# One step of a two-layer hybrid decoder on one core: boundary order, the last chunk's samples, states in the index keys' place, 25 projection blocks

## The reference, cut to what matters

```python
for l in range(DEPTH):
    mod = (silu_c @ p['w_ada'][l] + p['b_ada'][l]).reshape(B, N_MOD, D)
    hh = modulate(rmsnorm(x, g_pre[l, 0]), m[0], m[1])
    x = x + 0.5 * m[2] * rmsnorm(swiglu(hh, ...), g_post[l, 0])
    ...                      # mixer of the layer, then a second SwiGLU
```

```python
    inner = jnp.einsum('bhij,bjhv->bihv', att, vb)
    cross = jnp.einsum('bihd,bhdv->bihv', qb, s) * q_dec[None, :, :, None]
    s = s * c_dec[None, :, None, None] + jnp.einsum('bjhd,bjhv->bhdv', kb * k_dec[None, :, :, None], vb)
```

## Time and profile before

| what | value |
|---|---|
| median of 3 runs (lowest, highest) | 1372.47 us (1371.24, 1377.88) |
| the profiled execution's own time | 1372.95 us |
| its span (first to last instruction) | 1371.3 us |
| busy PE, DVE, ACT, POOL | 1333.3, 787.0, 623.6, 110.8 us |
| granted TensorE clock, mean | 0.998 of full |
| DMA | 260.00 MB, mean 190 GB/s |

### The profile page before, as it was taken

The page is one execution under the profiler, slowest core; times in us unless marked ns, Lnnn a source line. Parts: engine busy times, 40 slices in busy tenths (PEclk is TensorE's granted clock), DMA queues, the critical chain, the costliest instruction groups (busy, mean ns, idle before and its releaser), DMA issues.

```text
span 1371.3 us, 24418 instructions
## 1 busy us (share of the span) xinstructions
PE 1333.3 (97%) x9776; PEld 1254.5 (91%) x9776; DVE 787.0 (57%) x1432; ACT 623.6 (45%) x1068; POOL 110.8 (8%) x199
## 2 busy tenths in 40 slices
PE   6999999999999999999999999999998999999998
PEld 4899999989976789999999899999987989999997
DVE  5444444576787885445455644445576895444443
ACT  5433333463533555344344534334467665333332
POOL 0100000032011111000000200000020110000000
PEclk9999999999999999999999999999999999999999
DMA  9865646456359756554544546444564843444342
GB/s 361 300 213 188 214 159 241 154 172 225 123 201 349 279 196 224 183 186 142 200 149 158 209 146 227 154 167 158 168 221 141 293 154 123 153 150 147 127 146 83
DMA packets 79459, 260.00 MB, mean 190 GB/s; under 512 B 10626, under 2 KB 20930, under 8 KB 78210
## 3 DMA queue, kind: packets, MB, share of 16 engines
q1 hardware_dynamic: 62882, 199.50, 43.3%
q0 software_dynamic: 16480, 59.15, 11.8%
HBM read 254.39 MB, written 4.23 MB: 189 GB/s over the span
## 4 chain that ended last, share of the span: by engine, by line
PE 87%; DVE 5%; DMA 4%; ACT 2%; issue 1%; SPq 1%; POOL 0%; DVEq 0%; ACTq 0%
PE ps L1701 27%; PE ps L1702 26%; PE ps L1703 26%; PE ps L1769 2%; DMA lent_lo<-in_ada 2%; DMA front<-in_front 1%; DVE w_lo L2274 1%; DVE f L2359 1%; DVE f L2342 1%; DMA w_raw<-in_pj 1%; ACT w_hi L2052 1%; DVE x L2346 0%; DMA st_in<-in_state_ret 0%; DVE f L2364 0%; PE ps L1318 0%
## 5 line engine op out<-in xcount | busy, mean ns | idle before, releaser
L1701 PE MATMUL ps<-xn_hi,w_hi 128*128 128x320 f32 x1808 | 569.3, 315 | 11.7 <-DVE xn_lo L2354 7.5
L1703 PE MATMUL ps<-xn_hi,w_lo 128*128 128x320 f32 x1808 | 559.4, 309 | 0.0
L1702 PE MATMUL ps<-xn_lo,w_hi 128*128 128x320 f32 x1808 | 559.2, 309 | 0.0
L2274 DVE TENSOR_TENSOR w_lo<-w_raw,w_hi 128x1024 fp32r<-128x1024 f32 (+1 forms) x357 | 383.1, 1110 | 121.4 <-ACT w_hi L2052 120.9
L2052 ACT ACTIVATE w_hi<-w_raw 128x1024 fp32r<-128x1024 f32 x362 | 331.5, 961 | 81.7 <-PE ps L1703 74.3
L1701 PEld LDWEIGHTS ps<-xn_hi,w_hi 128*128 128x128 f32 x1808 | 340.0, 188 | 28.0 <-DVE xn_lo L2354 10.9
L1702 PEld LDWEIGHTS ps<-xn_lo,w_hi 128*128 128x128 f32 x1808 | 340.3, 188 | 0.9
L1703 PEld LDWEIGHTS ps<-xn_hi,w_lo 128*128 128x128 f32 x1808 | 340.0, 188 | 0.0
L1701 PE MATMUL ps<-mid_hi,w_hi 128*128 128x320 f32 x704 | 217.9, 310 | 0.3 <-DVE w_lo L2274 0.3
L1702 PE MATMUL ps<-mid_lo,w_hi 128*128 128x320 f32 x704 | 217.2, 308 | 0.0
L1703 PE MATMUL ps<-mid_hi,w_lo 128*128 128x320 f32 x704 | 217.2, 308 | 0.0
(11 more groups left out here) (321 smaller groups left out, 1045.1 us busy)
## 6 DMA issues: line engine op xcount, KB each, us to landing
w_raw<-in_gu SPq DMA_DIRECT2D x176, 512.0 KB, 4.7
a_raw<-in_ada POOLq DMA_DIRECT2D x76, 512.0 KB, 7.3
w_raw<-in_down SPq DMA_DIRECT2D x64, 512.0 KB, 3.6
w_raw<-in_pj SPq DMA_DIRECT2D x58, 512.0 KB, 5.0
w_raw<-in_down SPq DMA_DIRECT2D x64, 192.0 KB, 3.6
ex_xn<-in_ada POOLq DMA_DIRECT2D x16, 512.0 KB, 5.8
w_raw<-in_ada SPq DMA_DIRECT2D x16, 512.0 KB, 5.9
front<-in_front SPq DMA_DIRECT2D x5, 1024.0 KB, 12.4
```

What stands on the lines that cost most here:

```text
L1701: pe.matmul(out, hi, xhi, start=start, stop=False)
L1702: pe.matmul(out, hi, xlo, start=False, stop=False)
L1703: return pe.matmul(out, w_lo[s][:, w_at:w_at + P], xhi, start=False, stop=stop)
L2274: dve.tensor_tensor(w_lo[s][:, cols], w_raw[:, s, cols], w_hi[s][:, cols].bitcast(F32), ALU.subtract).then_inc(w_split, 1)
```

## The change

It has these parts. (1) Boundaries: `two_tiles` takes a written order (`FIRST_TILES`): after chunks 0 and 1 of tile 0 come chunks 0 and 1 of the first block of tile 1, then chunk 2 of tile 0 and the second block of tile 1; from chunk 4 on the order is the old one. (2) The last chunk's samples go from POOL to DVE: the scale stands before `low(6)`, the shift behind it. (3) even_in has 25 blocks: wi shares block 7 with ki (ACT writes three pieces out of it), rv of head 0 is block 9, the last tile is a half (and 8 columns, which the copy takes along). (4) The states of heads 0, 1 and 3 land where the index keys lay (`cached[:, :, 0, :]`), those of heads 0 and 1 from the fifth `ix_done` on, that of head 2 in `st_in`; SP's wait for `st_landed` goes. (5) `cross`: q times old state is made with 32 columns of q as weights and the state as the moving side, eight products into PSUM rows of 32, copied by ACT (`xs`), then two products with a selection matrix (`sel_x`, a new constant). (6) DVE's rounds for the samples: 1 at b = 22, then 4, 3, 1 in heads 0, 1, 2; at b = 24 the prompt's rounds and mask stand before the weight split. PE's `logits(0)` stands before the wait for all blocks. (7) odd_in: ACT loads the sigmoid's table ahead, and its `gates` stand before the weight splits. (8) gate0's first pieces stand at tile 2, not 3. (9) `out_projection`: ACT's wait for the gate factors stands behind the first weight split. (10) `stat_last`: the token sums stand before the products with x.

```diff
-EVEN_BLOCKS = 26
+EVEN_BLOCKS, EVEN_SLOTS = 25, 26
+HALF_TILE = 1024 + 8
+def even_slot(b):
+    if b == 9:
+        return B_RV
+    return b if b < B_RV else b + 1
-ADA_PLAN += [("gate0", c, 4) for c in (3, 7, 11, 15, 19)] + [("down0", 1, 4)]
+ADA_PLAN += [("gate0", c, 4) for c in (2, 7, 11, 15, 19)] + [("down0", 1, 4)]
+BOTH = (0, 1)
+FIRST_TILES = [(0, 0, BOTH), (0, 1, BOTH), (1, 0, (0,)), (1, 1, (0,)), (0, 2, BOTH), (1, 0, (1,)), (0, 3, BOTH),
+               (1, 1, (1,)), (0, 4, BOTH), (1, 2, BOTH), (0, 5, BOTH), (1, 3, BOTH), (0, 6, BOTH), (1, 4, BOTH),
+               (0, 7, BOTH), (1, 5, BOTH), (1, 6, BOTH), (1, 7, BOTH)]
-            for k in range(2, KC):
+            for k in range(2, KC - 1):
                 samples(gp, stage, k)
+        def state_of(h):
+            past = cached[:, :, 0, P * (h % 2):P * (h % 2 + 1)]
+            return st_in[:, :, :] if h == 2 else past
...
+            gp.wait_ge(ix_done, 5)
+            load_state(0)
+            load_state(1)
             gp.wait_ge(p_evac, PB + EVEN_BLOCKS)
             gp.wait_ge(rope_done, CR + 16)
+            gp.dma_start(t["k_o"], proj[:, B_K, :]).then_inc(kvo_stored, 16)
...
             for h in range(RH):
+                if h < RH - 2:
+                    gp.wait_ge(st_ready, h + 1)
+                    gp.wait_ge(o_done, h + 1)
+                    load_state(h + 2)
+                store_states(gp, h)
...
                 turn(2 * h)
+                pe.wait_ge(qd_ready, h + 2)
+                pe.wait_ge(st_landed[h % 2], 16 * (h // 2 + 1))
+                for b in range(NB):
+                    a, rows = b // 4, slice(32 * (b % 4), 32 * (b % 4 + 1))
+                    last = pe.matmul(ps[rows, a, 0:P], qz[:, NT * b:NT * b + 32], state_of(h)[:, b, :], start=True,
+                                     stop=True)
+                last.then_inc(xs_done, 1)
...
                 pe.wait_ge(vm_ready, h + 1)
+                pe.wait_ge(xs_ready, h + 1)
...
-                pe.wait_ge(st_landed, 16 * (h + 1))
-                for b in range(NB):
-                    pe.matmul(ps[:, 3, PTOK:TOK], st_in[:, b, :], qz[:, STOK * b:STOK * (b + 1)],
-                              start=(b == 0), stop=False)
+                for a in range(2):
+                    pe.matmul(ps[:, 3, PTOK:TOK], xs[:, a, :], sel_x[:, a, :], start=(a == 0), stop=False)
...
-            pe.wait_ge(p_evac, PB + EVEN_BLOCKS)
             pe.wait_ge(rope_done, CR + 16)
             logits(0)
+            pe.wait_ge(p_evac, PB + EVEN_BLOCKS)
...
+                    if b + h == B_KI:
+                        for to in (0, HD):
+                            act.activation(proj[to:to + HD, B_KI, :], ps[0:HD, 2 * j + h, 0:TOK], ACT.Copy)
+                        act.activation(proj[0:32, B_WI, :], ps[HD:HD + 32, 2 * j + h, 0:TOK], ACT.Copy).then_inc(p_evac, 1)
+                        continue
...
                 turned(2 * h)
+                act.wait_ge(xs_done, h + 1)
+                act.activation(xs[:, :, :], ps[:, 0:2, 0:P], ACT.Copy).then_inc(xs_ready, 1)
                 exponents(2 * h + 1)
...
+                if b == 24:
+                    top(scores[1], 2)
+                    mask(scores[1], bias_p[:, 1, :])
                 if b != 8:
                     n = base + b // 2 + (2 if b < 8 else 1)
-                    split_w(n, n % 2)
+                    split_w(n, n % 2, HALF_TILE if n == base + EVEN_IN_TILES - 1 else 2048)
...
-            dve.memset(qz[:, :], 0.0).then_inc(qd_ready, 1)
+            dve.memset(qz[:, STOK:STOK + 32], 0.0).then_inc(qd_ready, 1)
...
-                if h < 2:
-                    top(score_s[:, :], score_rounds // 3)
-                elif h == 2:
+                if h < RH - 1:
+                    top(score_s[:, :], late_rounds[h])
+                if h == RH - 2:
                     mask(score_s[:, :], bias_s[:, :])
...
             ada_copy(14)
+            act.activation(warm[:, :], eps[:, :], ACT.Sigmoid)
...
             evacuate_x(4)
+            gates(0)
             split_half(4, 0)
-            gates(0)
             evacuate_x(5)
             split_half(4, 1)
             gates(1)
+            gates(2)
             evacuate_x(6)
             split_half(5, 0)
-            gates(2)
             gates(3)
...
                             sp_.wait_ge(w_used, CR + W_BASE["even_out"])
-                            sp_.wait_ge(st_landed, 16)
...
             def stat_last(stage):
-                pe.wait_ge(x_ready, 8 * 5)
-                pe.wait_ge(row_ready, A_UNITS)
-                for k, bank in PE_ADDS.items():
-                    pe.matmul(ps[:, bank, 0:TOK], ident[:, :], x[:, k, :], start=True, stop=False)
                 pe.wait_ge(y_evac, CR + 8 * SUB[stage] + 7)
                 token_sums(B_YSUM, 0, sqacc[:, :], True, False)
                 pe.wait_ge(sq_ready, 8 * (SUB[stage] + 1))
                 token_sums(B_YSUM, 0, sq2[:, 1, :], False, True).then_inc(stat_done, 1)
+                pe.wait_ge(x_ready, 8 * 5)
+                pe.wait_ge(row_ready, A_UNITS)
+                old(0)
                 spread(y_stat(stage), ry3, B_RY)
+                old(1)
+                grown(0)
...
             def out_projection(stage, done):
-                act.wait_ge(coef_ready, 2 * SUB[stage] + 2)
...
+                    if i == 0:
+                        act.wait_ge(coef_ready, 2 * SUB[stage] + 2)
                     act.wait_ge(half_used, done + i + 1)
...
                         scaled(k)
+                        if k == KC - 1:
+                            sample_scale(k)
                         low(k - 1)
+                    dve.wait_ge(xmod_ready, 8 * sub + KC - 1)
+                    sample_shift(KC - 1)
                     low(KC - 1)
```

More of the change, by code:

```diff
@@ L315, in build @@
         sel_s = pb("sel_s", [P, 2, STOK])
+        sel_x = pb("sel_x", [P, 2, STOK])
         hmask = pb("hmask", [P, NIH])
@@ L365, in build @@
         w_used = sem("w_used")
-        fr_landed = [sem(f"fr_landed{c}") for c in range(KC)]
         fr_row, fr_sel, fr_mod = sem("fr_row"), sem("fr_sel"), sem("fr_mod")
@@ L898, in evacuate @@
                 if t_:
-                    split_w(base + t_ + 1, (base + j + 1) % 2)
-                for h in range(2):
-                    if h == 0:
+                    split_w(base + t_ + 1, (base + j + 1) % 2, HALF_TILE if t_ + 2 == EVEN_IN_TILES else 2048)
+                for h in range(len(kinds)):
+                    if h == 0 and len(kinds) == 2:
                         act.wait_ge(half_used, t_ + 1)
@@ L917, in act_even @@
             for b in range(0, EVEN_BLOCKS, 2):
-                kinds = ((plain, key) if B_RQK <= b < B_RQK + 8 else
-                         ((ACT.Silu, 1.0),) * 2 if b >= B_RG else (plain, plain))
+                kinds = tuple(key if B_RQK <= q < B_RQK + 8 and q % 2 else
+                              (ACT.Silu, 1.0) if even_slot(q) >= B_RG else plain
+                              for q in range(b, min(b + 2, EVEN_BLOCKS)))
                 evacuate(b // 2, b // 2 % 2, b, kinds)
@@ L1645, in proj_loads @@
                 for i in tiles:
-                    load_w(t["pj"], first_tile + i, W_BASE[stage] + i)
+                    half = stage == "even_in" and i == EVEN_IN_TILES - 1
+                    load_w(t["pj"], first_tile + i, W_BASE[stage] + i, HALF_TILE if half else 2048)
             def lent_loads():
@@ L1736, in two_tiles @@
                         pe.wait_ge(xn_ready, 8 * PREP[stage] + k + 1)
-                    for b in range(2):
+                    for b in blocks:
                         if k == 0:
@@ L1891, in stat_last @@
                 token_sums(B_YSUM, 0, sq2[:, 1, :], False, True).then_inc(stat_done, 1)
+                pe.wait_ge(x_ready, 8 * 5)
+                pe.wait_ge(row_ready, A_UNITS)
+                old(0)
                 spread(y_stat(stage), ry3, B_RY)
-                for k, bank in PE_ADDS.items():
-                    pe.wait_ge(y_grown, k + 1 + k % 2)
-                    pe.matmul(ps[:, bank, 0:TOK], ident[:, :], f[:, k, :], start=False, stop=True).then_inc(y_sum, 1)
+                old(1)
+                grown(0)
+                old(3)
+                grown(1)
+                grown(3)
             def ff_sums(stage):
@@ L2761, in tables @@
     out["sel_s"], out["rep_s"] = sel, sel.transpose(2, 1, 0)
+    out["sel_x"] = sel * (xx == 0)[:, None, None]
     head = 2 * (xx % 2) + xx // 2
```

99 lines of the change are left out of this document (50 added, 49 removed).

## The result

The changed kernel takes 1360.03 us (median of 4 runs, 1357.74 to 1360.75), the kernel before on the same chip 1372.95 (4 runs, 1371.24 to 1377.88). The ratio is 0.990, 95% interval 0.987 to 0.9925.

What follows compares the result with a forecast made beforehand. PE, busy 97% of the span, bounds the kernel. Terms -1.2 - 3.5 - 0.75 - 4.2 - 0.4 - 5.3 - 1.6 + 1.25 = -15.7 us on 1372.95 give 1357.25, forecast as 1356.8 for the median; range 1352 to 1361.5.

Steps and rivals of the forecast that it cites:

- Boundaries: At five boundaries: the written order removes no wait, and chunk 7's scale delays low(6); +0.25 us each, +1.25 in all.
- gate0: Before gate0's tile 2: 16 moved products fill PE's idle 1.12 us and its short stall; -1.2 us.
- even_in and the entry: even_in: one block less, -3.5 us; entry to the heads: fewer DVE rounds and less memset before logits(0), -0.75 us.
- The heads: Attention heads: cheaper cross -3.6, no waits for w_ada pieces -1.2, DVE's later rounds and states +0.6; -4.2 us.
- rival (a): Attention stage: the DMA queue binds, PE keeps a 0.6 us wait in two heads; +1.3, 1358.1 us; chance 0.14.
- even_out: Before even_out's second tile: PE's 1.27 us wait for a bank shrinks as ACT and DVE split sooner; -0.4 us.
- odd_in: odd_in: gate waits go, -3.6 us, and the time lost to a lowered clock behind them, -1.7; -5.3 us.
- The table load: odd_in: ACT's 1.28 us sigmoid table load fits in 1.35 us of idle time, delaying the next high part 0.2 at most.
- The end: Kernel end: 1.61 us of products no longer stand before the token sums; -1.6 us.
- (b): Boundaries: each gains 0.44 us from the written order instead of losing 0.25; 1353.3 us; chance 0.13.
- (c): odd_in: DVE's 31 us run starts when it did and holds back the 5.3 us gain; 1362.1 us; chance 0.10.
- (d): Attention stage: TensorE's clock falls, making the kernel slower than before, 1417 us if throughout; chance 0.03.

Runs made afterwards that it cites:

- experiments 9 and 10: The kernel before with only chunk 7's samples moved to DVE, and the kernel before with only part 7: ratios to before 1.0005 and 0.9975.
- experiments 1 and 2: Changed kernel with chunk 7's samples back on POOL, median 1357.39 us; changed kernel with low(6) ahead of sample_scale(7), median 1357.94 us.
- experiment 3: Changed kernel with two_tiles in the old order at the boundaries, chunk 7's samples still on DVE: median 1359.73 us, ratio to before 0.990.
- experiment 8: Changed kernel with the old products of q with the old state and the wide qz memset: median 1362.40 us, ratio to before 0.993.
- Part 7 alone: The kernel before with only part 7 (sigmoid table loaded ahead, gates ahead of weight halves): median 1368.50 us, ratio to before 0.9975.
- odd_undone: Changed kernel with part 7 undone (no early sigmoid table load, gates behind the weight halves): median 1362.65 us, odd stretch 113.14 us.
- odd_no_order: Changed kernel with the early sigmoid table load kept but the gates behind the weight halves again: median 1361.48 us, odd stretch 112.22 us.
- before_part2: The kernel before with only chunk 7's samples moved to DVE at all five boundaries: median 1372.14 us, ratio to before 1.0005.
- experiments 5 to 7: Changed kernel with part 7 undone, without its early table load, and without its new gate order: medians 1362.65, 1361.62 and 1361.48 us.
- odd_no_table: Changed kernel without the early load of the sigmoid's table, gates in their new order: median 1361.62 us, odd stretch 110.50 us.
- best2: best1 with added products on PE at the start to warm it: median 1361.12 us.
- best1: Changed kernel with low(6) ahead of sample_scale(7) and head 2's state loaded early into the relu buffer: median 1358.92 us, ratio to before 0.992.

## Why the prediction came out right, and where it did not

It forecast 1356.8 us with a range of 1352.0 to 1361.5; the median is 1360.0. Its sum against the profiled execution, 15.7 us less, stands beside a measured 15.2, of which 0.8 is the start of the kernel and not the change: 14.4 us are left. That the two totals lie within 0.5 us is in part luck: the heads gave 1.5 less than forecast, and 0.6 more in odd_in and 0.8 at the start made up for it. Of the 14.4, some 1.5 to 3 are what the profiled execution of the kernel before had to lose and most others had not (experiments 9 and 10), which leaves a usual worth of 11.5 to 13 us. The medians say 12.9, or 11 to 13 with the later medians of the kernel before (1370.99 to 1373.03). Point by point:

- **Boundaries** (+0.25 each): right in place and size. gate1 and gate2, which nothing else touches, grew by 0.28 and 0.27; experiments 1 and 2 take it away again. It was also right that the written order earns nothing (experiment 3 finds 0.02 us), but the wait did not move as forecast: PE still idles before chunk 3 (0.62 us, 0.53 before), where the forecast had that wait go to chunk 4; there 0.26 is new; what went is the wait before chunk 2 (0.61).
- **gate0** (-1.2): -1.4. Tile 2 starts 2.10 us behind its predecessor's last matmul instead of 1.42, with 16 products between, and tile 3's are gone.
- **even_in and the entry** (+0.25 - 3.5 - 0.75 = -4.0): from the second reciprocal to k x v of head 0 it is 112.10 us where it was 116.14: -4.04. PE's two waits at the entry, 0.53 us for ACT's last copy (at 397.13) and 0.58 for `am_s`, are one of 0.22 now: 0.89 us less, where 0.75 was forecast. The memset's 0.5 inside that term is not borne out (experiment 8).
- **The heads** (-4.2): -2.7, the step that failed. Two terms of it were mis-sized. The new product saves 0.57 us a head and not 0.9: the two selection products take 0.59 instead of 0.48, and two seams around the new product take 0.1 each that no row of before could show. And the waits for pieces did not go: of 2.0 us that the queue cost, 1.4 stayed, and since other executions of both show 1.0 to 2.3, even the 0.6 is not safe. The prediction counted bytes against PE's time (14.9 us against 14.3) and then trusted the lead; the windows of the changed kernel show a queue that is never free (DMA share 1.01). It ran faster than the 356 GB/s of the sum: at 393 a head's 5.3 MB take 13.5 us, just under the 13.8 to 15.1 from one head's k x v to the next (394.99, 408.82, 423.92, 438.82), so the count of bytes alone does not give these waits. This is rival (a), with about the price that it named (1.3). The 0.3 us for DVE's added round in head 0 did not show.
- **even_out** (-0.4): -0.15 (from `turn` of the last head to the next reciprocal, 40.13 to 39.98). PE's wait for the bank is 1.11 us instead of 1.27.
- **odd_in** (-5.3, with the boundary -5.05): -5.64 in the profiled pair, and right in its mechanism: no wait, clock at 1.00. Part 7 alone is worth 5.93 against that execution: 3.6 of waits, 0.8 of restarts behind three waits, which the prediction left out (`odd_undone`'s 2.78 less its 2.0 of waits; `odd_no_order` has 1.86 for 1.3 of two waits), and 1.5 for the half clock, where the prediction had 1.7. But it is worth 2.8 in the changed kernel, and 1.9 to 4.9 by time in the kernel before. The step that failed is taking one execution's longest wait, and the half clock behind it, for every execution's: the half is late by 0.6 to 1.4 us in three traces, and the times leave little room for the half clock in most executions. Beside the heads this is why the median is 3.2 us above the forecast. The prediction also did not see that part 2 alone makes the half land in time (`before_part2`, 2.91 us off the stretch in its profiled execution); with part 7 in place that adds nothing, so the sum does not change by it.
- **The table load** hid where it was put: in the changed kernel it starts at 1007.68 us, the activation behind it 1.29 later (1008.97), and the high part at 1009.40, for which ACT then waited 0.22 us on PE. The drain of 1.38 us of the Trainium skill ("ScalarE: Activation LUTs", on what a table load costs) doesn't show here either.
- **The end** (-1.6, with the boundary -1.35): -1.04. The last reciprocal comes 1.94 us behind the last large matmul instead of 3.35: 1.41 gained, and what remains is the boundary's.

Rivals (b), (c) and (d) did not come about: for (b) see experiment 3, for (c) experiments 5 to 7, and against (d) the clock in the heads is 1.00.

## What to carry to other kernels

Where an engine binds chunk by chunk, ask of each added operation which chunk's product stands behind it, not how long it is: chunk 7's scale costs 0.25 us ahead of `low(6)` and nothing behind it. Where the bytes of a loop take as long as the loop, a lead is used up before it ends, and an earlier transfer only moves the wait; take bytes out, or give PE's gain no credit for the waits. A wait that ends on a DMA can have another length in each execution, and the clock behind it need not fall in most: time the part alone before crediting it in full.

## What the runs showed of the hardware

**The clock fell behind one wait of PE, and not behind shorter ones in the same place.** In the profiled execution of the kernel before, ACT waited 1.51 us for a weight half, PE then 2.28 for ACT, and the granted clock fell to half (1.2 of 2.4 GHz) for a part of the next 10 us (0.76 on average from 1030 to 1035 us, 0.90 from 1035 to 1040). With a first wait of 0.66 or 0.68 us and a second of 1.05 it stayed full (`odd_undone`, `before_part2`). It is one execution in which the clock fell there.

**Arithmetic on an idle engine can set the time of a DMA.** POOL's two small operations on chunk 7 hold back 3.1 MB of its piece loads by 1.85 us (15.24 against 13.40 and 13.39 us behind the reciprocal). A 512 KB load that SP issues at about 20 us then takes 7.5 to 8.4 us in all three traces and not the 5.6 to 7.0 of the eleven others.

**The start scatters by up to 8 us.** From the first to the second reciprocal the profiled executions took 266.4 to 274.3 us, whatever the kernel. Two windows of the first microseconds, of the changed kernel and of `odd_no_table`:

```profile
20.00:25.00 5.00, 4.10 (x45) 2.52 (x45) 4.23 (x14) 4.31 (x7) 0.00 (x0) 1.00 1.03 428
```

```profile
20.00:25.00 5.00, 4.50 (x27) 2.83 (x26) 2.10 (x7) 1.67 (x4) 0.00 (x0) 0.50 1.03 428
```

In the second the clock is at half and 27 products get done where 45 did; it came back to full between 35 and 40 us. `odd_no_order`, 272.0 us in this stretch, shows a clock of 1.00 in the column, but each four of its `front_turn` products take 1.02 us like those at half clock, against 0.61; so durations tell more than the column there. The page of one execution can mislead by microseconds in the first 40; stretches behind them were compared for this reason. What decides when the full clock comes was not found: more work for PE at the start (`best2`) went with full speed from 13.7 us in the profiled execution, but `best1` had the same without it, and the median is no shorter.
